# A block-matrix attention kernel: the fifth and seventh block product of each half pair written as 512-column matmuls

## What is computed

```python
proj = u @ w_in                      # 512x2048 @ 2048x8192: q | k | v | z
a = softmax(q0 k0 + bias) - lam * softmax(q1 k1 + bias)     # per head pair
o = rms_norm(a @ v) * (1 - lam_init)
h = layer_norm(ALPHA * x + (o * silu(z)) @ w_out)
```

## Time and profile before

| what | value |
|---|---|
| time, median of 3 runs | 876.25 us |
| the profiled execution's own time | 876.08 us |
| its span, first to last instruction | 874.3 us |
| outside the span | 1.8 us |
| TensorE matmuls, busy | 866.6 us, 5050 instructions |
| VectorE busy | 710.1 us |
| ScalarE busy | 454.6 us |
| granted TensorE clock | 1.000, full speed (2.4 GHz) in all of the span |

### The profile page before, as it was taken

One profiled execution on the slowest core, in us unless ns is written; L12 is line 12 of the kernel. 1 busy time (PEld: TensorE's weight loads), 2 busy tenths in 40 slices (PEclk: granted clock), 3 DMA queues, 4 the chain that ended last, 5 costly groups with the idle time before them and its releaser, 6 DMA issues.

```text
span 874.3 us, 14306 instructions
## 1 busy us (share of the span) xinstructions
PE 866.6 (99%) x5050; PEld 769.4 (88%) x5050; DVE 710.1 (81%) x1072; ACT 454.6 (52%) x695; POOL 281.4 (32%) x496
## 2 busy tenths in 40 slices
PE   9999999999999999999999999999999999999997
PEld 8888899999999999999989898989898978888886
DVE  5686778897888788878988898889788986976986
ACT  4445555545555555555555554555556563655511
POOL 1301516151606150525152515251424215130033
PEclk9999999999999999999999999999999999999999
DMA  8822685777587677757685768576857765997733
GB/s 298 317 84 80 143 221 117 218 177 201 116 241 168 184 149 237 151 174 162 226 159 172 166 219 163 171 167 192 172 151 176 275 225 145 231 180 245 273 123 115
DMA packets 54092, 161.38 MB, mean 185 GB/s; under 512 B 9760, under 2 KB 11808, under 8 KB 53808
## 3 DMA queue, kind: packets, MB, share of 16 engines
q0 software_dynamic: 24928, 71.37, 40.2%
q1 hardware_dynamic: 24720, 80.49, 25.8%
q10 hardware_dynamic: 4416, 9.18, 3.1%
HBM read 143.66 MB, written 13.15 MB: 179 GB/s over the span
## 4 chain that ended last, share of the span: by engine, by line
PE 96%; DVE 2%; DMA 0%; issue 0%; ACT 0%; SPq 0%; DVEq 0%; ACTq 0%
PE proj L1760 50%; PE att L1760 46%; DMA w_raw<-w_in_tiles_dram 0%; DVE w_split L1182 0%; DVE w_split L1166 0%; DVE scratch L1342 0%; DVE big L1752 0%; DVE scratch L1369 0%; ACT scratch L907 0%; DVE scratch L1325 0%; DVE last_stats L1738 0%; DVE operands L1320 0%; DVE x_res L1226 0%; DVE xg_split L1489 0%; DVE proj L1263 0%
## 5 line engine op out<-in xcount | busy, mean ns | idle before, releaser
L801 ACT ACTIVATE w_split<-w_raw 128x1024 fp32r<-128x1024 f32 x196 | 206.9, 1059 | 157.0 <-PE proj L1760 85.7
L1166 DVE TENSOR_TENSOR w_split<-w_raw,w_split 128x1024 fp32r<-128x1024 f32 x196 | 238.2, 1218 | 52.0 <-ACT w_split L801 51.0
L1760 PE MATMUL att<-w_split,xg_split 128*128 128x512 f32 (+1 forms) x832 | 170.8, 361 | 0.0
L1760 PEld LDWEIGHTS att<-w_split,xg_split 128*128 128x128 f32 x832 | 142.4, 189 | 24.3
L691 POOL DMA_DIRECT2D scratch<-scratch x256 | 127.7, 593 | 41.8 <-DVE scratch L1369 32.4
L1760 PE MATMUL proj<-w_split,xg_split 128*128 128x256 f32 (+1 forms) x800 | 137.4, 330 | 1.4 <-DVE operands L1320 0.7
L1760 PEld LDWEIGHTS proj<-w_split,xg_split 128*128 128x128 f32 x800 | 120.5, 190 | 15.8 <-DVE operands L1320 1.2
L1760 PE MATMUL proj<-xg_split,w_split 128*128 128x256 f32 (+1 forms) x752 | 126.4, 327 | 0.3 <-DVE w_split L1509 0.3
L1760 PEld LDWEIGHTS proj<-xg_split,w_split 128*128 128x128 f32 x752 | 112.0, 191 | 12.8 <-issue 0.6
L714 POOL DMA_DIRECT2D w_raw<-w_in_tiles_dram x84 | 73.9, 889 | 130.3 <-DVE w_split L1166 101.5
L1760 PE MATMUL proj<-w_split,sums 128*128 128x256 f32 (+1 forms) x656 | 103.5, 317 | 0.0
(11 more groups left out here) (191 smaller groups left out, 1020.6 us busy)
## 6 DMA issues: line engine op xcount, KB each, us to landing
w_raw<-w_in_tiles_dram SPq DMA_DIRECT2D x98, 512.0 KB, 4.2
w_raw<-w_in_tiles_dram POOLq DMA_DIRECT2D x84, 512.0 KB, 5.8
w_raw<-w_out_tiles_dram SPq DMA_DIRECT2D x19, 512.0 KB, 3.7
w_raw<-w_out_tiles_dram POOLq DMA_DIRECT2D x12, 512.0 KB, 8.1
bias_by_distance<-bias_lines POOLq DMA_DIRECT2D x8, 640.0 KB, 6.1
scratch<-scratch POOLq DMA_DIRECT2D x128, 40.0 KB, 2.8
bias<-bias_by_distance POOLq DMA_DIRECT2D x8, 512.0 KB, 4.1
scratch<-scratch POOLq DMA_DIRECT2D x128, 32.0 KB, 2.0
```

The source lines that it names most:

```text
L801: nc.scalar.activation(split_view(a, 0), pair_raw(a), ACT.Copy).then_inc(w_hi, 1)
L1166: nc.vector.tensor_tensor(split_view(a, 1), pair_raw(a), split_view(a, 0).bitcast(F32), ALU.subtract).then_inc(w_ready, 1)
L1760: return nc.tensor.matmul(dst, lhsT, rhs, start=start, stop=stop, skip_group_check=True)
```

## The change

Steps 4 and 6 get the wide form as well. Step 4's product now stands in both halves of the two banks: ScalarE copies the low half to a new SBUF tile `kept_seventh`, VectorE adds the other half to it (`keep_seventh`), and `finish_upper` and `finish_corner` take the sum from SBUF. Step 6's halves are added by VectorE in two passes in `finish_lower`, and the write of the lower block now waits for the second.

```diff
+        kept_seventh = sb("kept_seventh", [P, 2, PW])
...
         def wide_banks(h, step):
-            if step in (0, 3):
+            if step in (0, 3, 6):
                 return half_banks(h, 0)
+            if step == 4:
+                return half_banks(h, 1)
...
+            def take_seventh_low(p, h):
+                act.wait_ge(quarter_done, slots_before(p) + h * PHASE + 5 * BLOCKS)
+                nc.scalar.activation(kept_seventh[:], wide_banks(h, 4)[:, :, 1], ACT.Copy).then_inc(seventh_low, 1)
...
                     take_fifth_low(p, h)
+                if r == 5 * BLOCKS:
+                    take_seventh_low(p, h)
                 split_hi_at(p, j)
...
+            def keep_seventh(p, h):
+                dve.wait_ge(seventh_low, phase_number(p, h) + 1)
+                nc.vector.tensor_tensor(kept_seventh[:], wide_banks(h, 4)[:, :, 0], kept_seventh[:], ALU.add
+                                        ).then_inc(seventh_kept, 1)
...
             def finish_upper(p, h):
                 dve.wait_ge(fifth_less, phase_number(p, h) + 1)
-                dve.wait_ge(quarter_done, slots_before(p) + h * PHASE + 5 * BLOCKS)
                 dve.wait_ge(third_kept, phase_number(p, h) + 1)
+                dve.wait_ge(seventh_kept, phase_number(p, h) + 1)
                 nc.vector.tensor_tensor(region_of(h, 1), kept_third, kept_fifth, ALU.add).then_inc(upper_done, 1)
             def finish_corner(p, h):
-                dve.wait_ge(quarter_done, slots_before(p) + h * PHASE + 5 * BLOCKS)
-                nc.vector.tensor_tensor(kept_sum, kept_sum, region_of(h, 4), ALU.subtract).then_inc(sum_less, 1)
-                nc.vector.tensor_tensor(region_of(h, 4), region_of(h, 4), kept_fifth, ALU.add).then_inc(corner_done, 1)
+                nc.vector.tensor_tensor(kept_sum, kept_sum, kept_seventh[:], ALU.subtract).then_inc(sum_less, 1)
+                nc.vector.tensor_tensor(region_of(h, 4), kept_seventh[:], kept_fifth, ALU.add).then_inc(corner_done, 1)
...
             def finish_lower(p, h):
...
-                nc.vector.tensor_tensor(region_of(h, 6), region_of(h, 6), kept_first, ALU.add).then_inc(upper_left_done, 1)
+                halves = wide_banks(h, 6)
+                nc.vector.tensor_tensor(kept_first, halves[:, :, 0], kept_first, ALU.add).then_inc(upper_left_begun, 1)
+                dve.wait_ge(upper_left_begun, phase_number(p, h) + 1)
+                nc.vector.tensor_tensor(region_of(h, 6), halves[:, :, 1], kept_first, ALU.add).then_inc(upper_left_done, 1)
+                dve.wait_ge(upper_left_done, phase_number(p, h) + 1)
                 nc.vector.tensor_tensor(region_of(h, 5), wide_banks(h, 5)[:, :, 1], kept_sum, ALU.add).then_inc(lower_done, 1)
...
                 if r == 5 * BLOCKS:
+                    keep_seventh(p, h)
                     finish_upper(p, h)
                     finish_corner(p, h)
...
-                opens = c == 0 and step in (4, 6)
+                opens = c == 0 and step == 4
...
-WIDE = {0: None, 1: 2, 2: 0, 3: None, 5: 0}
+WIDE = {0: None, 1: 2, 2: 0, 3: None, 4: None, 5: 0, 6: None}
```

More of the change, by code:

```diff
@@ L268, in diff_layer @@
         sum_begun = sem("sum_begun")
+        upper_left_begun = sem("upper_left_begun")
+        seventh_low = sem("seventh_low")
+        seventh_kept = sem("seventh_kept")
         upper_left_done = sem("upper_left_done")
```

## The result

| | before | after |
|---|---|---|
| median, 4 runs each on the same chip | 876.32 us | 891.49 us |
| ratio, 95% interval | | 1.0169 (1.0157 to 1.0181) |
| the profiled execution | 876.08 us | 891.28 us |
| its span | 874.3 us | 889.5 us |
| TensorE matmuls | 5050 | 4602 |

The change makes the kernel slower, as forecast, but by 15.2 us where 4.1 were forecast, and 9.0 us above the top of the range. Lines of the kernel after: L1783 is the matmul (L1760 before), L807 and L1179 are the weight splits of ScalarE and VectorE (L801, L1166), L1347 moves z out (L1325), L1342 moves v out (L1320), L1251 is the VectorE part of `keep_third` (L1238), L697 GpSimd's swaps (L691), L720 its weight additions (L714), L1364 the maxima of a score tile (L1342), L1396 VectorE's turn of the gated output (L1374), L943 ScalarE's `g_copy`, which reads the swapped tile (L932), L579 SyncE's weight loads (L573).

The account below looks back on a forecast made before the run. TensorE was taken to bound the kernel, with VectorE's list from the scores to z only 0.38 us shorter. Matmuls -2.2, six changes of pair +4.5 and the end +1.8 gave +4.1 us: 880.3 us, range 877.4 to 882.5.

Parts of the forecast that it names:

- Part 1, the matmuls: Wide steps 4 and 6 on TensorE: 0.16 us saved a step, 28 steps, 4.5 us if nothing else binds.
- Rival 3: The wide form saves nothing in steps 4 and 6, so -2.2 us falls away: 882.5 us; chance 0.05.
- Part 2, the list of h = 1: VectorE's list up to moving z out: copy 0.25, `keep_seventh` 0.60, own-engine wait 0.12, sum +0.97 us.
- signal and restart: At step 0 behind a late z: TensorE resumes 0.10 us after the event, loses up to 0.1 refilling; 0.15 taken.
- The end of pair 7: VectorE's list grows by 0.97 and 0.84 us, so row tile 2 of the output projection starts 1.8 us later.
- h = 0: First half pair: VectorE's additions covered, 1.97 us spare at slot 14; wide steps save 0.32 us a pair, -2.2 us.
- the pause ahead of score tile 2: VectorE's idle time there, 1.27 us usually and 0.93 in pair 2, takes up what remains late.
- The term for a change of pair: Step 0 of the next pair waits for z and starts 0.75 us later; six times, +4.5 us.
- Rival 4: A second wait at slot 3's weights: a split 1.5 us later costs 0.7 more a boundary, 884.5 us; chance 0.04.

Follow-up runs that it names:

- h1_only: The changed kernel with steps 4 and 6 wide in the h = 1 half pairs only: 884.30 us, 1.0093 of the kernel before.
- h0_only: The changed kernel with steps 4 and 6 wide in the h = 0 half pairs only: 881.01 us, 1.0056 of the kernel before.
- h0_loads_wait: Steps 4 and 6 wide in h = 0 only, SyncE's loads after step 4 of h = 1 held until the last weight addition landed: 875.08 us, 0.9983.
- pool_delay: The kernel before, no wide step 4 or 6, four memsets delaying GpSimd ahead of its swaps by about 2.4 us a pair: 891.21 us, 1.0181.
- step4_only: The changed kernel with step 4 wide in both half pairs and step 6 plain: 883.80 us, 1.0084 of the kernel before.
- after_both: The changed kernel with SyncE's loads held until the last weight addition landed and z moved out one split earlier: 881.36 us, 1.0071.

## Why the prediction was wrong

**Part 1, the matmuls: right.** 32 matmuls in 5.59 us in the chain for steps 4 and 6 (in the timeline 5.75 with the tail), 28 steps save 4.7 us by the slots' lengths where 4.5 was forecast. The page's gap rule ("TensorE: Matmul & The Clock Gate" of the Trainium skill, section "Back-to-back issue gap") would have given 28 x 0.04, an estimate of 1.1; the trace disagrees. That section gives the rule for an isolated matmul and says itself that a stream with weight loads keeps another distance, so it was no firm rival here. Rival 3 is out.

**Part 2, the list of h = 1: right within 0.2 us a change.** h1_only shows it alone. `keep_seventh` starts at 350.79 and `finish_upper` 0.81 later, not 0.72, so a pass with an own-engine wait cost 0.2 more than one without (0.61); the rule of the Trainium skill, "VectorE: DVE Perf Modes", section "The DRAIN you can't avoid", that a semaphore costs nothing extra there, is not what this trace shows. For signal and restart together I took 0.15 us. By starts, step 0 behind a pause takes 5.69 us (182.71 to 188.40) where it took 5.58 (353.86 to 359.44), 0.11 more, and the signal takes 0.13 (L1347 ends 358.95, the matmul starts 359.08): 0.24 in all.

**The end of pair 7: 2.0 us for 1.8.** From the scores of tile 2 to row tile 2 of the output projection are 26.04 us (691.49 to 717.53), before 24.08 (678.28 to 702.36). The 2.3 us above are the stalls alone and leave out what steps 4 and 6 save there. It is the same list, with the same two small terms.

**h = 0: this step failed.** The prediction said that "VectorE's additions in h = 0 are covered", checked against slot 14 only (1.97 us to spare, of which 1.04 was to go; in pair 2 TensorE waits there for 0.18 us, so even this margin did not hold), and that "What remains late is taken up by the pause ahead of score tile 2". h0_only costs 4.7 us instead of bringing 2.2. That path is what failed: I had followed VectorE's lateness to TensorE and not to GpSimd. GpSimd's swaps start 0.3 us after the end of VectorE's turn of the gated output, before as after (395.11 + 1.24 to 396.64, 403.04 + 1.24 to 404.58 in pair 4), and the weight additions follow by two ways, behind the swaps in the same queue and behind ScalarE's `g_copy`. Late additions meet SyncE's loads and take 1.2 us longer by h0_only against h0_loads_wait; they also follow each other closer. pool_delay shows the loop without the change; h0_loads_wait shows that without the collision h = 0 comes to 875.08, 1.2 us below before. That is half of the 2.2 us that I had put down.

**The term for a change of pair also failed from there.** It was anchored at score tile 2, as if VectorE always arrived there in time and with its weights ready. In pair 3 it arrived with 0.19 us of idle left and lost 1.15 us on the way to a weight split. The pauses grew from 1.0 (h1_only) to between 1.03 and 1.98 us.

**Slot 19 was missed.** It lies ahead of the pause on which I relied, and had only 0.4 us to spare in pair 2. Rival 4 had the right idea, a second wait, at the wrong place: slot 3's weights never showed.

**The clock had no term.** 4.7 us of the 15.2 are what three stretches at 1.2 GHz cost. Neither h0_only nor h1_only has one among its changes of pair, so this part exists only where both ways add up: 7.2 us of span in h1_only and 5.4 in h0_only make 12.6, the whole change has 15.2. I count it with the pauses as observed together; no run held the pause fixed and varied the clock.

## What to carry to other kernels

When an engine gets more work, follow its lateness to every reader, also to the one with 32% busy time, and on through that reader's queue: what stands behind it (here DMA additions of weights that are due a few slots later) may be due at the engine that started it. A pause that takes up lateness covers only what comes behind it, so list the tightest margin at each wait between the edit and the pause. And run the edit's halves alone: h1_only showed one term of the forecast right to 0.2 us and h0_only showed the other wrong in sign, which the full change could not.

## What the hardware showed that was not expected

- After idle times of 1.98, 1.76 and 1.96 us ahead of step 0, TensorE's granted clock was 0.50 for 3.41 us and the next 32 matmuls took 7.40 instead of 5.85 us. After 1.47, 1.25 and 1.03 us at the same place it stayed at 1.00, and also after 2.10 us ahead of the output projection, where 12 matmuls took 3.00 us as in the earlier trace rows. In step4_only the clock fell once, at that place, after 2.51 us, and in after_both at that place after 2.11 us, where the kernel after kept 1.00 with 2.10. So the length of one pause alone doesn't decide.
- A weight addition that a split waited for took 10.5 us from issue to split with SyncE's loads beside it and 9.3 us without; in the chain of pair 5 the addition alone is 10.75. Holding the loads of the other queue back, from 2.3 to 9.4 us behind the addition, cost nothing.
- 2.4 us of delay a pair on GpSimd cost 14.8 us of 876, though the engine is busy for a third of the time.
